# Attention values: a head's high and low halves side by side in one stationary tile

## What is computed

```python
s = jnp.where(mask, s + bias, NEG_INF)
p = jnp.exp(s - m)
den = p.sum(-1, keepdims=True)
o = jnp.einsum('bhrnqk,bhrnkd->bhrnqd', p, vs.astype(jnp.float32)) / den   # heads 0..15
...
p = jax.nn.softmax(s, axis=-1)
return jnp.einsum('bhrqk,bhrkd->bhrqd', p, v_blk.astype(jnp.float32))      # heads 16..31
```

## Time and profile before

| | |
|---|---|
| time, median of 3 runs | 2238.85 us (2238.75 to 2239.31) |
| the profiled execution | 2238.29 us, span 2236.5 us |
| PE busy | 2224.2 us, 99% (10378 matmuls) |
| weight loads busy | 1850.1 us, 83% |
| VectorE busy | 1264.8 us, 57% |
| ScalarE busy | 990.9 us, 44% |
| GpSimd busy | 225.3 us, 10% |
| the three lines of the projections (L1348 to L1350) | 31% of the chain each |
| the values matmuls (L1436) | 192 matmuls, 1% of the chain |
| scores (L1408, L1412), turned probabilities (L1422) | 192 and 128 matmuls |
| attention, from the first v2 evacuation to the last values job | 1792 to 2105 us |

### The profile page before, as it was taken

The page is one execution under the profiler, slowest core; times in us unless marked ns, Lnnn a source line. Parts: engine busy times, 40 slices in busy tenths (PEclk is TensorE's granted clock), DMA queues, the critical chain, the costliest instruction groups (busy, mean ns, idle before and its releaser), DMA issues.

```text
span 2236.5 us, 24480 instructions
## 1 busy us (share of the span) xinstructions
PE 2224.2 (99%) x10378; PEld 1850.1 (83%) x10378; DVE 1264.8 (57%) x1029; ACT 990.9 (44%) x950; POOL 225.3 (10%) x253
## 2 busy tenths in 40 slices
PE   9999999999999999999999999999999999999998
PEld 8888888888888888888888888888888888888886
DVE  6577645546555545555544544454555577676655
ACT  7465654333333443444433433333444455555542
POOL 1023010000000000000000100000100132253201
PEclk9999999999999999999999999999999999999999
DMA  9554456777787766655556556555556755556663
GB/s 321 183 181 161 166 182 199 211 222 223 233 238 229 212 207 204 224 180 184 185 194 193 182 196 192 187 190 188 188 188 203 242 191 174 188 169 184 210 232 118
DMA packets 217069, 444.91 MB, mean 199 GB/s; under 512 B 9284, under 2 KB 10452, under 8 KB 216064
## 3 DMA queue, kind: packets, MB, share of 16 engines
q1 hardware_dynamic: 206944, 411.07, 56.2%
q0 software_dynamic: 9728, 32.18, 6.2%
q10 hardware_dynamic: 288, 0.10, 0.0%
HBM read 427.08 MB, written 12.06 MB: 196 GB/s over the span
## 4 chain that ended last, share of the span: by engine, by line
PE 99%; DMA 0%; DVE 0%; POOL 0%; ACT 0%; issue 0%; POOLq 0%; SPq 0%
PE acc L1348 31%; PE acc L1349 31%; PE acc L1350 31%; PE side L1358 2%; PE side L1436 1%; PE side L1372 1%; PE side L1408 1%; PE side L1422 1%; DMA raw<-in_w_in 0%; PE side L1393 0%; PE side L1391 0%; PE side L1392 0%; PE side L1458 0%; PE side L1459 0%; POOL X L652 0%
## 5 line engine op out<-in xcount | busy, mean ns | idle before, releaser
L942 DVE TENSOR_TENSOR wlo<-raw,whi 128x2048 fp32r<-128x2048 f32 x380 | 892.5, 2349 | 751.3 <-ACT whi L669 751.0
L669 ACT ACTIVATE whi<-raw 128x2048 fp32r<-128x2048 f32 x380 | 727.9, 1916 | 783.3 <-PE acc L1350 758.2
L1348 PE MATMUL acc<-whi,setA_lo 128*128 128x512 f32 x1792 | 700.4, 391 | 0.6 <-DVE wlo L974 0.6
L1350 PE MATMUL acc<-whi,setA_hi 128*128 128x512 f32 x1792 | 697.4, 389 | 0.0
L1349 PE MATMUL acc<-wlo,setA_hi 128*128 128x512 f32 x1792 | 697.4, 389 | 0.0
L1348 PE MATMUL acc<-whi,setB_lo 128*128 128x512 f32 x1280 | 502.9, 393 | 0.0
L1349 PE MATMUL acc<-wlo,setB_hi 128*128 128x512 f32 x1280 | 498.8, 390 | 0.0
L1350 PE MATMUL acc<-whi,setB_hi 128*128 128x512 f32 x1280 | 498.3, 389 | 0.0
L1350 PEld LDWEIGHTS acc<-whi,setA_hi 128*128 128x128 f32 x1792 | 336.3, 188 | 70.3
L1348 PEld LDWEIGHTS acc<-whi,setA_lo 128*128 128x128 f32 x1792 | 336.4, 188 | 70.0 <-issue 1.1
L1349 PEld LDWEIGHTS acc<-wlo,setA_hi 128*128 128x128 f32 x1792 | 336.5, 188 | 68.5
(11 more groups left out here) (206 smaller groups left out, 1012.4 us busy)
## 6 DMA issues: line engine op xcount, KB each, us to landing
raw<-in_w_in SPq DMA_DIRECT2D x188, 1024.0 KB, 5.2
raw<-in_w_ffn_up SPq DMA_DIRECT2D x64, 1024.0 KB, 5.2
raw<-in_w_ffn_down SPq DMA_DIRECT2D x64, 1024.0 KB, 5.1
raw<-in_w_gla_out SPq DMA_DIRECT2D x16, 1024.0 KB, 5.1
raw<-in_w_conv_out SPq DMA_DIRECT2D x16, 1024.0 KB, 5.1
raw<-in_w_o SPq DMA_DIRECT2D x16, 1024.0 KB, 5.2
raw<-in_w_out SPq DMA_DIRECT2D x16, 1024.0 KB, 5.1
t_scratch<-t5v POOLq DMA_DIRECT2D x8, 512.0 KB, 7.2
```

What stands on the lines that cost most here:

```text
L669: e.activation(whi[r][:, :, :], raw[r][:, :, :], ACT.Copy).then_inc(s_hi, 1)
L942: e.tensor_tensor(wlo[r][:, :, :], raw[r][:, :, :], asf(whi[r][:, :, :]), ALU.subtract).then_inc(s_lo, 1)
L1348: e.matmul(o, xl, whi[r][:, k, :], start=kk == 0, stop=False)
L1350: f = e.matmul(o, xh, whi[r][:, k, :], start=False, stop=kk == 15)
```

## The change

A head's hi and lo columns stand side by side in one stationary tile of 128 columns, vs[g][s][:, head, :] (one tile for each key block; s = 0 in the region where vhi was, s = 1 where vlo was). One matmul with moving PTl and one with moving PT give, in the upper 64 partitions of the output, hi x (lo + hi of the probabilities), and in the lower 64, lo x (the same); lo x lo, which was left out before, comes along. The two halves of 64 rows are then added. ScalarE copies one half from the bank into YT (L895, L896 as before, now with an increment of the new semaphore s_yv), VectorE adds the other half, in add_halves(p), and this addition releases the bank. In VectorE's program add_halves(p) stands at the head of the job ("att", a) with a = 2p+4, behind split(s+2); add_halves(15) stands in a = 33. Both parts of a v2 tile are written with a stride, and the wait for scores 23 is moved from VectorE to ScalarE.

```diff
-        vhi = [at(f"vhi{g}", "W", 4 * KB * (g % 2), [128, 2, 512], f32r) for g in range(4)]
-        vlo = [at(f"vlo{g}", "A", (16, 20, 16, 24)[g] * KB, [128, 2, 512], f32r) for g in range(4)]
+        vs = [[at(f"vs{g}0", "W", 4 * KB * (g % 2), [128, 8, 128], f32r),
+               at(f"vs{g}1", "A", (16, 20, 16, 24)[g] * KB, [128, 8, 128], f32r)] for g in range(4)]
...
@@ ScalarE, post() of a v2 unit
+                    if j == 3:
+                        e.wait_ge(*full("scores", 23))
                     e.wait_ge(s_rstd, 3)
                     for t in range(2):
-                        e.activation(vhi[j][:, t, :], acc[u % 2][t][:, :], ACT.Copy,
+                        e.activation(vs[j][t][:, :, 0:64], acc[u % 2][t][:, :].rearrange("p (h d) -> p h d", h=8), ACT.Copy,
                                      scale=rstd[2][:, t:t + 1]).then_inc(s_vh, 1)
...
@@ ScalarE, att, odd a
-                            e.activation(YT[0:64, p, :], side[n % 4][0:64, 0:256], ACT.Copy)
-                            e.activation(YT[64:128, p, :], side[n % 4][0:64, 256:512], ACT.Copy).then_inc(s_read[n % 4], 1)
+                            e.activation(YT[0:64, p, :], side[n % 4][64:128, 0:256], ACT.Copy).then_inc(s_yv, 1)
+                            e.activation(YT[64:128, p, :], side[n % 4][0:64, 256:512], ACT.Copy).then_inc(s_yv, 1)
...
@@ VectorE, post() of a v2 unit
-                    if j == 3:
-                        e.wait_ge(*full("scores", 23))
                     for t in range(2):
                         e.wait_ge(s_vh, 2 * j + t + 1)
-                        e.scalar_tensor_tensor(out=vlo[j][:, t, :], in0=acc[u % 2][t][:, :], scalar=rstd[2][:, t:t + 1],
-                                               in1=asf(vhi[j][:, t, :]), op0=ALU.mult, op1=ALU.subtract).then_inc(ev, 1)
+                        e.scalar_tensor_tensor(out=vs[j][t][:, :, 64:128],
+                                               in0=acc[u % 2][t][:, :].rearrange("p (h d) -> p h d", h=8),
+                                               scalar=rstd[2][:, t:t + 1], in1=asf(vs[j][t][:, :, 0:64]), op0=ALU.mult,
+                                               op1=ALU.subtract).then_inc(ev, 1)
...
@@ VectorE
+            def add_halves(p):
+                n = SN["values", p]
+                e.wait_ge(s_yv, 2 * p + 2)
+                for i in range(2):
+                    rows = slice(64 * i, 64 * i + 64)
+                    c = e.tensor_tensor(YT[rows, p, :], side[n % 4][rows, 256 * i:256 * i + 256], YT[rows, p, :], ALU.add)
+                c.then_inc(s_read[n % 4], 1)
...
                     elif job == "att":
+                        if a % 2 == 0 and a >= 4:
+                            add_halves(a // 2 - 2)
+                        if a == 33:
+                            add_halves(15)
...
@@ TensorE, values(p)
-                        for n, (x, y) in enumerate(((vlo[g], PT), (vhi[g], PTl[g]), (vhi[g], PT))):
-                            f = e.matmul(bank[0:64, 256 * i:256 * i + 256],
-                                         x[:, s, 128 * j + 64 * i:128 * j + 64 * i + 64],
-                                         y[i][:, s, :], start=s == 0 and n == 0, stop=s == 1 and n == 2)
+                        for n, y in enumerate((PTl[g], PT)):
+                            f = e.matmul(bank[:, 256 * i:256 * i + 256], vs[g][s][:, 2 * j + i, :], y[i][:, s, :],
+                                         start=s == 0 and n == 0, stop=s == 1 and n == 1)
```

More of the change, by code:

```diff
@@ L344, in two_block_program @@
         s_pn, s_ph, s_pl = sem("s_pn"), sem("s_ph"), sem("s_pl")
-        s_vh, s_yh, s_yl = sem("s_vh"), sem("s_yh"), sem("s_yl")
+        s_vh, s_yv, s_yh, s_yl = sem("s_vh"), sem("s_yv"), sem("s_yh"), sem("s_yl")
         s_var, s_sd, s_rs, s_nmu = sem("s_var"), sem("s_sd"), sem("s_rs"), sem("s_nmu")
```

## The result

| | before | after |
|---|---|---|
| median | 2238.68 us (9 runs) | 2245.26 us (9 runs, 2244.78 to 2247.33) |
| ratio | | 1.0031, 95% interval 1.0022 to 1.0040 |
| profiled execution | 2238.29 us, span 2236.5 | 2245.29 us, span 2243.4 |
| PE waits on VectorE's additions | none | 11, 9.4 us |

The change makes the kernel 0.3% slower, 6.6 us. 2241.5 was predicted, with "no difference" as the likeliest sign; the forecast of what is saved and where PE would wait came true. The size of the ordinary waits did not, and behind the two long waits the clock fell, which the sum had at nothing.

The account below looks back on a forecast made before the run. PE's instruction stream was taken as the bound: 7.3 us saved, against 0.4 for loads, 2.7 ordinary waits, 3.3 and 4.05 long waits, less 0.5, gives +2.6 us on 2238.85, so 2241.5 us; 8 in 10 range 2235.5 to 2245.5.

Parts of the forecast that it names:

- no difference: Likeliest sign of the whole kernel's time, between 2234.4 and 2243.3 us: chance 0.57, against slower 0.33 and faster 0.10.
- what is saved: In the 16 values jobs, 8 matmuls instead of 12, 64 fewer at 0.114 us: 7.3 us saved, 0.46 per job.
- ordinary waits: In twelve steps (p = 0 to 11) PE waits for the late bank, up to 0.5 us each: 2.7 us, range 1.0 to 4.5.
- the clock: Rival, chance 0.10: after each of two long pauses TensorE's clock falls, up to 2.0 us each, 2243.5 to 2245.5 us.
- the sum: Over the whole kernel, -7.3 + 0.4 + 2.7 + 3.3 + 4.05 - 0.5 = +2.6 us.
- What bounds it: PE's instruction stream is the time: work leaving it shortens the kernel in full, waits lengthen it in full.
- The wide tile: In values jobs, loading 128 stationary columns instead of 64 mostly hides behind the matmul before: 0.4 us, between 0 and 0.8.
- The late release: VectorE's add_halves frees the bank in step a = 2p+4 behind L942; PE resumes at L942's end + 0.76 us.
- none before values 15: At step a = 32, PE's old wait for PTl before values 15 vanishes: -0.5 us.
- The wait of step 28: At the scores of step a = 28 (p = 12), ScalarE's table load and Silu make VectorE's split late: 3.3 us.
- That of step 30: Inside the probs of step a = 30 (p = 13), VectorE is later still, behind turn_y: 4.05 us.
- The rival by which that chain slides with PE: Chance 0.12: VectorE's work of step 29 hangs on PE, second wait grows by up to 2.1 us: 2243.6 to 2245.4 us.

Follow-up runs that it names:

- two_products: The kernel before without its product of vlo and PT, 64 fewer narrow matmuls, bank still released by ScalarE: 2232.99 us, ratio 0.9974.
- adds_hoisted: The changed kernel with add_halves(p) still in its even step but ahead of split(s+2): 2238.04 us, ratio 0.9992 to the kernel before.
- small_bias_add: The changed kernel with GpSimd's addition of mask and bias cut from 256 to 8 columns per tile: 2242.93 us, ratio 1.0019.
- late_release: The kernel before with its 12 narrow matmuls per job, bank released by two VectorE operations behind the even step's split: 2249.74 us, ratio 1.0048.
- adds_odd: The changed kernel with add_halves(p) moved to the odd step a = 2p+3, behind that step's split: 2235.21 us, ratio 0.9984.
- y_copy: The changed kernel with a plain copy in place of the y units' Silu, so without ScalarE's table loads: 2244.80 us, ratio 1.0027.

## Why the prediction was half right

**What bounds it, and that PE's time is worth its full length:** right. 14 jobs of two_products gained 0.453 us each against 0.457 forecast.

**The wide tile (0.4 us between 0 and 0.8):** eight matmuls now stand 0.119 apart (0.95 us a job), as in the earlier trace rows, so it lies near the upper bound: 0.038 x 16 = 0.6 us. The rule of the Trainium skill (TensorE: Matmul & The Clock Gate, section "The mechanism", and not the section that the prediction names) that a load overlaps a running matmul only in another row group doesn't describe this case: loads of 128 columns cost 0.005 us more per matmul, not 0.057.

**The late release:** right in its place. The waits are at exactly the jobs named, nine ordinary ones, the scores of step 28 and the second probs of step 30, and none before values 15. (At a = 10 and 26, forecast at nothing, the scores come 0.2 and 0.1 us later.) Moving the additions removed them, but for the one of step 30 in adds_hoisted.

**The ordinary waits (2.7 us) are the step that failed:** 6.0 us. Two things are in it. First, each wait was worked out some 0.15 us too low: the pair of additions takes 0.85 us and not 0.74 (they don't overlap as the L1301 pair does), and PE comes 0.14 and not 0.10 after them; nine times that is the 1.3 us that small_bias_add leaves. My upper end of 4.5 had that. Second, I had treated VectorE's split as 2.29 to 2.43 us in these steps, as it was in the rows read. That GpSimd's addition stretches it, by up to 0.85 us in the changed kernel, was to be seen before: the earlier trace rows show only 0.14 us of it, but the splits of steps beside them took up to 3.19 us in the same trace:

```profile
1851.22 1.28 POOL L563 TENSOR_TENSOR bia<-bia,msk 128x512 f32<-128x512 f32 x1 [3.02 <-DMA bia<-t_scratch]
...
1851.46 3.19 DVE L942 TENSOR_TENSOR wlo<-raw,whi 128x2048 fp32r<-128x2048 f32 x1 [0.80 <-ACT whi L669]
```

In the changed kernel such an overlap fell on splits that the bank hangs on (a = 4 and a = 12: 0.95 and 1.15 us instead of 0.14 and 0.27). Why on these is open: late_release, whose values jobs are as long as before, has it at a = 4 too (a split of 2.97 us, 0.97 us lost) and hardly at a = 12 (2.36 us, 0.35 us lost).

**The wait of step 28 (3.3 us):** 3.0. **That of step 30 (4.05 us):** 2.45, and the missing 1.6 are the clock's loss before it. The forecast of VectorE's time there was right: counted from PE's probs of step 28, its split comes 0.7 us later than before. The rival by which that chain slides with PE was wrong.

**The clock is the second step that failed:** the sum had it at nothing. A rival with a chance of 0.10 and a price of up to 2.0 us a pause came true: 1.6 and 1.4 us, of which one lies on the path (in other executions a single pause lost up to 2.7). I had no row of a pause, and gave the rule on pauses too little weight. The Trainium skill (TensorE: Matmul & The Clock Gate, "HAM oscillation") has it that pauses between bursts throttle the array. Here the trace agrees, with 0.53 of the granted clock over 3.3 us, though the pauses are shorter than those of that page's example, and behind others of 1.7 and 2.3 us the clock stayed full.

**The sum:** forecast +2.6. 0.3 us less is saved (+0.3), ordinary waits +3.3, wait of step 28 -0.3, its clock +1.6, wait of step 30 -1.6, its clock +1.4, the wait before values 15 -0.2: +7.1 against 6.9 measured on the span. So of the 4.5 us between +2.6 and +7.1, 3.3 are the ordinary waits and 1.4 the clock; the rest nearly cancels.

## What to carry to other kernels

Where a bank or buffer changes hands to another engine, the cost is the place in that engine's program at which it is released, against the place of the next use: number the uses, and compare the two times step by step, with the worst step decisive. A saving on the bound engine is full only until it reaches the next resource that was released just in time; here 0.3 us of slack at one bank took 1.3 to 1.8 us of 6. And add to every new pause of TensorE what its clock may lose behind it (here 1.0 to 2.7 us), unless a later wait takes that up. Where GpSimd and VectorE work side by side, look at the longest record of an instruction and not only at the one in the step that you work out.

## What the runs showed of the hardware

- The idle time that the profile gives before a matmul understates its price: it counts from the modelled end. The wait before the fifth transpose of step a = 8 reads 0.47 us, while the start-to-start distance grew by 0.63.
- The granted clock fell to 1.2 GHz behind the pauses of 2.9 and 2.2 us of the changed kernel (0.53 over 3.3 us, 0.64 to 0.69 over 5.2) and stayed at 1.00 behind one of 1.7 (adds_odd) and one of 2.3 (y_copy), so the length of the pause alone doesn't tell it. It fell some 1.6 us after PE had resumed from the first, and 0.5 us after it had from the second; in a pause of 3.7 us in y_copy it fell before PE resumed at 2088.46 us (0.65 from 2086 to 2089), and was at 0.50 in the 3 us behind. What was lost behind one pause was 1.0 us (late_release, adds_hoisted) to 2.7 us (small_bias_add, 0.50 over 6.8 us).
- A GpSimd addition of 128 x 512 beside VectorE's subtraction of 128 x 2048 stretches that from 2.29 to 2.8 and 3.1 us; with the addition cut to 16 columns no split in the attention took more than 2.294 us. Which of the two starts first decides: over the attention of the twelve traces with the full addition, 164 of 177 splits were stretched that an addition already running overlapped (up to 3.43 us; the other 13 shared 0.2 us or less with it), and none of 97 that had started before the addition (2.27 to 2.29 us). There the addition took longer instead, as the 2.92 us in step 28 above, and up to 3.4 us where it takes 1.3 alone.
